# The first expert weights of the odd tiles wait for the first two row gathers, in a decoder step with a grouped mixture of experts

## The chip, the cores and the metric

The kernel runs on one core of one Trainium2 chip. The metric is the device time of one execution in microseconds (us), and lower is better.

## What is computed

One inference step of a one-layer hybrid decoder for 1024 prompt tokens and 32 sample tokens (8 sequences of 4), with a model width of 1024, all in float32. A combined input projection feeds forgetting attention, sparse attention with a window, and an HGRN2 recurrence. An output projection, a residual sum and a layer norm follow. Then comes the part in which the change lies, a grouped top-2 mixture over 16 experts of hidden width 256:

```python
def moe_block(x, router_w, router_bias, w1, w3, w2):
    xf = x.reshape(B * T, D)
    comb = route(xf, router_w, router_bias)        # two experts of one group for each token
    hgt = jnp.einsum('nd,edf->nef', xf, w1)
    hup = jnp.einsum('nd,edf->nef', xf, w3)
    hh = jax.nn.silu(hgt) * hup * comb[..., None].astype(x.dtype)
    return jnp.einsum('nef,efd->nd', hh, w2).reshape(B, T, D)
```

A last residual sum and layer norm give the outputs.

## The kernel before

The program is written out by hand, one instruction stream for each engine, with semaphores between them. SyncE (SP) issues nearly all loads, GpSimd (POOL) issues the stores and the indirect gathers. "arena" in the trace is one large SBUF allocation that holds nearly every tile; "act" and "vec" are rings of PSUM banks, named after the engine that empties them.

The mixture stage computes only the chosen experts. Each token is copied twice, the copies are sorted by expert, and each expert's copies are padded to halves of 64 rows. There are 48 halves, cut into four streams of 12 (`SEG`). A tile is two halves, so there are 24 tiles: an even tile takes one half of stream 0 and one of stream 2, an odd tile one of stream 1 and one of stream 3. Each stream has a slot of its own for the gate and up weights (`Wgu`, 2 MB) and one for the down weights (`Wd`, 1 MB). What each engine does for tile k:

- POOL gathers the tile's 128 token rows of 4 KB from the DRAM tensor `x1_rows` into `xg[k % 2]` (`fetch`, L2035) and counts `x0_loaded` or `x1_loaded` up by 16. `fetch(0)` and `fetch(1)` are issued as soon as DVE has the row numbers (L1903). `fetch(k + 2)` waits until TensorE has turned tile k.
- TensorE turns the rows (`turn_rows`, L1066), eight transposes. It waits for the gather and, from tile 1 on, until ACT (L1322) and DVE (L1920) have emptied the banks of the tile before. It then multiplies by gate and up weights (`gate_up`, L1086, 32 matmuls), which wait for the weights of both streams, and later by the down weights (`down`, L1099).
- TensorE's order is: turn tile 0, turn tile 1, gate_up of tile 0, then in a loop turn tile k + 2, turn the hidden values of tile k, gate_up of tile k + 1, down of tile k. So gate_up of tile 0 stands behind both first gathers, and gate_up of tile 1 needs the weights of streams 1 and 3.

SP's part of it: stream 0 always begins with expert 0, and its three loads go out before the routing is known. The first loads of the other three streams wait until DVE has the expert numbers ("experts known", L1886). `load_gate_up` issues two DMAs of 1 MB, whose contiguous pieces are 1 KB (L437). `load_down` issues one of 1 MB in pieces of 4 KB (L441). The number of the expert is read into a register before (`value_load`, L559). The loads of later steps (`next_gate_up`, `next_down`) are conditional on a change of expert, and wait for `gu_filled` and `dn_filled`, which TensorE counts.

Of the kernel before, what the change touches and what calls it, by code (L numbers as in the profile page):

```python
# [214 lines left out]
def program(nc, ctx, I, O_, known):  # L215
# [194 lines left out]
    def turned_tiles(d):  # L410
# [4 lines left out]
    msem = {n: ctx.enter_context(nc.semaphore(f"moe_{n}")) for n in  # L415
            ("x0_loaded", "x1_loaded", "gu0_loaded", "gu1_loaded", "gu2_loaded", "gu3_loaded", "d0_loaded", "d1_loaded", "d2_loaded", "d3_loaded", "xt_filled", "xt_by_act", "xt_by_vec", "gu_filled", "exp_done",
             "silu_steps", "hidden_done", "ht_filled", "ht_done", "dn_filled", "y_by_act", "y_by_vec", "y0_stored", "y1_stored")}
# [12 lines left out]
    def at_position(stream, j):  # L430

        return bass.ds(j + stream * SEG, 1)

    def load_gate_up(e, stream, expert, **only):
        slot, one = (stream + 1) % 4, bass.ds(expert, 1)
        for dst, src in ((Wgu[:, slot, :, 0:FE], I["exp_w1"]), (Wgu[:, slot, :, FE:], I["exp_w3"])):
            e.dma_start(dst, src[0, one].rearrange("e (c p) f -> p (e c) f", p=P), **only).then_inc(msem[f"gu{stream}_loaded"], 16)  # L437

    def load_down(e, stream, expert, **only):
        slot, one = (stream + 1) % 4, bass.ds(expert, 1)  # L440
        e.dma_start(Wd[:, slot], I["exp_w2"][0, one].rearrange("e (c p) f -> p (e c) f", p=P), **only).then_inc(msem[f"d{stream}_loaded"], 16)  # L441
# [3 lines left out]
    def _(e):  # L445
# [112 lines left out]
        def expert_at(stream, j):  # L558
            return e.value_load(ek_int[0:1, at_position(stream, j)], min_val=0, max_val=NE - 1)  # L559
# [3 lines left out]

        for stream in (2, 1, 3):
            expert = expert_at(stream, 0)
            load_gate_up(e, stream, expert)
            load_down(e, stream, expert)

# [34 lines left out]
    def _(e):  # L603
# [215 lines left out]
        def transposes(d):  # L819
            h, i, kinds = PAIRS[d]  # L820
            e.wait_ge(*E.at(("probs", d)))
            for j, kind in enumerate(kinds):
                _, L, nb = unit_keys(kind, i)
                for a in range(0, nb, 4):
                    e.wait_ge(*E.free("turned"))
                    bk = E.bank("turned")
                    for c in range(min(4, nb - a)):
                        n = min(P, L)
                        last = e.transpose(bk[:n, c * P:(c + 1) * P], score_tiles(d)[j][:, (a + c) * P:(a + c) * P + n], ident)  # L829
                    last.then_inc(*E.filled("turned", ("probs turned", d)))  # L830
# [296 lines left out]
    def _(e):  # L1127
# [131 lines left out]
        for it in range(n + 4):  # L1259
            d = it - 4  # L1260
            if d >= 0 and d % 2:
                h, i, _ = PAIRS[d]
                e.wait_ge(*E.full("summed"))
                bk = E.job("summed")
                e.copy(QT[:, h, i * P:(i + 1) * P], bk[:, 0:P]).then_inc(*E.drained("summed", "prompt attention done"))
            d = it - 2
            if 0 <= d < n:
                h, i, kinds = PAIRS[d]
                for j, kind in enumerate(kinds):
                    _, L, nb = unit_keys(kind, i)  # L1270
                    w = min(P, L)
                    for a in range(0, nb, 4):
                        k = min(4, nb - a)
                        e.wait_ge(*E.full("turned"))
                        bk = E.job("turned")
                        if d >= 2:
                            e.wait_ge(*E.at(("values", d - 2)))
                        e.copy(turned_tiles(d)[j][:w, a:a + k, :], bk[:w, 0:k * P].rearrange("p (c n) -> p c n", c=k)).then_inc(*E.drained("turned", ("pt", d, j)))  # L1278
            if it < n:
                h, i, kinds = PAIRS[it]  # L1280
                for j, kind in enumerate(kinds):
                    _, L, _ = unit_keys(kind, i)
                    e.wait_ge(*E.at(("scores", it, j)))
                    s, sm_ = score_tiles(it)[j][:, 0:L], small[:, it % 4]
                    act(s, s, ACT.Exp, scale=-1.0, bias=sm_[:, least(i, kind, j):least(i, kind, j) + 1], accum_out=sm_[:, j:j + 1]).then_inc(*E.done(("exps", it)))  # L1285
# [805 lines left out]
```

## Time and profile before

| | |
|---|---|
| median of 3 runs | 1565.12 us (1564.02 to 1570.11) |
| profiled execution, its own time | 1562.96 us |
| its span, first to last instruction | 1561.1 us |
| granted TensorE clock, mean over the span | 0.900 of full speed |
| TensorE matmuls busy | 1330.6 us (85%) |
| VectorE, ScalarE, GpSimd busy | 704.5, 376.5, 229.8 us |
| the chain that ended last, by engine | PE 70%, DVE 17%, DMA 4%, POOL 3% |
| mixture stage, from the first dynamic weight load to the last down matmul | 1178.3 to 1487.7 us |

Times in the trace count from the start of the span. The span is 1.9 us shorter than the execution's own time, and the table's median is 2.2 us above that time. The profile gives a DMA issue on SP or POOL as an instruction; how long it takes there is the time to hand the transfer over, and not the transfer. Queue q1 carries what SP issues, queue q0 what POOL issues. A DMA share is the packets' time over that of 16 DMA engines, and can pass 100% since packets overlap.

### The profile page before, as it was taken

The page shows a single profiled execution, that of the slowest core. Times are in us where ns is not written, and L with a number is a line of the kernel's source. Part 1 is how long each engine was busy: PE and PEld are TensorE (multiplying, and loading weights), DVE is VectorE, ACT ScalarE, POOL GpSimd, SP SyncE. Part 2 cuts the span into 40 slices and gives each one's busy share as a digit, 9 for nine tenths or more (in the row PEclk, how much of TensorE's full clock was granted, in tenths as well). Part 3 has the DMA queues.
Part 4 walks back from the last instruction along what each step waited for, and adds up shares of the span by engine and source line. Part 5 has one row for each costly group of instructions (what it writes and reads, how often), then busy time and mean ns, then how long its engine had stood idle before and what let it go on. Part 6 is the DMA issues. An engine that isn't in the chain of part 4 may idle for free.

```text
span 1561.1 us, 19466 instructions
## 1 busy us (share of the span) xinstructions
PE 1330.6 (85%) x7079; PEld 839.1 (54%) x7079; DVE 704.5 (45%) x1543; ACT 376.5 (24%) x817; POOL 229.8 (15%) x251
## 2 busy tenths in 40 slices
PE   2899999999999997899899688599954999999910
PEld 1577777878775555566566577244452333333300
DVE  6444666648541124655555411032643333433359
ACT  3222422324220002566466200000100111111111
POOL 0021030212110003223222100000001111111140
PEclk9799999999999996999999875799956999999965
DMA  9702020301112216000000300701228697595663
GB/s 321 214 1 54 29 55 16 68 1 30 54 42 88 37 18 166 8 23 24 1 2 1 109 0 6 243 0 41 77 102 286 229 323 238 189 314 169 242 222 137
DMA packets 114402, 163.14 MB, mean 105 GB/s; under 512 B 20931, under 2 KB 87667, under 8 KB 114328
## 3 DMA queue, kind: packets, MB, share of 16 engines
q1 hardware_dynamic: 100008, 112.73, 23.7%
q0 software_dynamic: 14320, 49.41, 9.0%
q8 instruction: 48, 0.79, 0.2%
q14 instruction: 26, 0.21, 0.1%
HBM read 225.00 MB, written 36.45 MB: 167 GB/s over the span
## 4 chain that ended last, share of the span: by engine, by line
PE 70%; DVE 17%; DMA 4%; POOL 3%; issue 2%; SPq 2%; ACT 1%; DVEq 0%; POOLq 0%; ACTq 0%
PE act L632 14%; PE vec L1086 10%; PE vec L1030 8%; PE vec L661 6%; PE vec L682 4%; DVE arena L1655 3%; POOL arena L2020 3%; PE vec L817 2%; PE act L841 2%; PE act L829 2%; PE act L1099 2%; PE vec L1099 2%; PE act L1020 2%; DVE arena L1963 1%; DVE arena L1378 1%
## 5 line engine op out<-in xcount | busy, mean ns | idle before, releaser
L632 PE MATMUL act<-arena 128*128 128x352 f32 x768 | 238.9, 467 | 0.4 <-issue 0.4
L632 PEld LDWEIGHTS act<-arena 128*128 128x128 f32 x768 | 145.4, 193 | 77.0 <-issue 3.5
L1086 PE MATMUL vec<-arena 128*64 128x512 f32 x768 | 173.4, 604 | 5.7 <-DMA arena<-in_exp_w 3.0
L1030 PE MATMUL vec<-arena 128*128 128x512 f32 (+1 forms) x288 | 128.1, 607 | 19.0 <-DMA arena<-in_w_out 19.0
L1655 DVE CUSTOM_DVE_ANT_0 arena<-vec,arena 128x128 f32<-128x128 f32 (+9 forms) x200 | 86.9, 458 | 99.8 <-PE vec L817 89.7
L1086 PEld LDWEIGHTS vec<-arena 128*64 128x64 f32 x768 | 54.7, 138 | 107.7 <-issue 107.3
L1030 PEld LDWEIGHTS vec<-arena 128*128 128x128 f32 (+1 forms) x288 | 52.7, 184 | 92.2 <-issue 91.3
L661 PE MATMUL vec<-arena 128*128 128x512 f32 (+1 forms) x256 | 99.9, 546 | 0.0
L817 PE MATMUL vec<-arena 64*128 64x512 f32 (+11 forms) x352 | 86.5, 491 | 2.5 <-DVE arena L1655 2.0
L1278 ACT COPY arena<-act 128x512 f32<-128x512 f32 (+11 forms) x176 | 63.5, 432 | 101.4 <-PE act L829 101.4
L2020 POOL TENSOR_SCALAR arena<-arena 128x640 f32<-128x640 f32 (+4 forms) x64 | 59.9, 947 | 185.6 <-DVE arena L1667 185.6
L1926 DVE TENSOR_SCALAR arena<-arena 128x256 f32<-128x256 f32 x24 | 7.1, 296 | 176.0 <-ACT arena L1328 176.0
L1285 ACT ACTIVATE arena<-arena 128x640 f32<-128x640 f32 (+15 forms) x128 | 81.6, 645 | 11.6 <-DVE arena L1655 11.5
L829 PE MATMUL act<-arena 128*128 128x128 f32 (+4 forms) x440 | 66.1, 287 | 21.0 <-POOL arena L2020 19.6
L661 PEld LDWEIGHTS vec<-arena 128*128 128x128 f32 x256 | 47.8, 190 | 44.9 <-issue 27.7
L829 PEld LDWEIGHTS act<-arena 128*128 128x128 f32 (+4 forms) x440 | 47.1, 142 | 43.1 <-POOL arena L2020 23.6
L682 PEld LDWEIGHTS vec<-arena 128*128 128x128 f32 x512 | 61.9, 192 | 9.3 <-DVE arena L1472 3.2
L1489 DVE COPY_PREDICATED arena<-arena,vec 128x512 f32<-128x512 int32 x64 | 44.7, 732 | 48.3 <-PE vec L682 46.5
L642 PE MATMUL vec<-arena 128*128 128x128 f32 (+1 forms) x576 | 65.3, 275 | 0.0
L642 PEld LDWEIGHTS vec<-arena 128*128 128x128 f32 (+1 forms) x576 | 64.5, 183 | 1.3
L682 PE MATMUL vec<-arena 128*128 128x128 f32 x512 | 62.7, 276 | 2.4 <-DVE arena L1472 2.4
L817 PEld LDWEIGHTS vec<-arena 64*128 64x128 f32 x352 | 43.3, 203 | 35.6 <-issue 24.7
(363 smaller groups left out, 1942.5 us busy)
## 6 DMA issues: line engine op xcount, KB each, us to landing
arena<-in_exp_w SPq DMA_DIRECT2D x144, 1024.0 KB
y_rows<-arena POOLq DMA_DIRECT2D x48, 256.0 KB, 5.3
arena<-in_w_in SPq DMA_DIRECT2D x16, 512.0 KB, 7.0
arena<-in_x_prompt SPq DMA_DIRECT2D x8, 512.0 KB, 10.4
x_spill<-arena POOLq DMA_DIRECT2D x8, 512.0 KB, 4.0
arena<-in_cache_fox_kv SPq DMA_DIRECT2D x16, 256.0 KB, 3.0
arena<-x_spill SPq DMA_DIRECT2D x8, 512.0 KB, 17.9
x_rows<-arena POOLq DMA_DIRECT2D x8, 512.0 KB, 3.6
```

What stands on the lines that cost most here:

```text
L632: last = mm(bk[:, 0:n], W[k % 2][:, c, m * P:(m + 1) * P], xT[:, c, a:a + n], start=c == 0, stop=c == NC - 1)
L642: last = mm(bk[:r, o:o + P], xT[:, c, t * P:t * P + r], W[h % 2][:, c, 3 * P:4 * P], start=c == 0, stop=c == NC - 1)
L661: last = mm(bk[:r, 0:width], xT[:, c, t * P:t * P + r], w[:, c, 0:width], start=c == 0, stop=c == NC - 1)
L682: last = mm(bk[:, c * P:(c + 1) * P], a[:, ch], b[:, ch], start=True, stop=True)
L817: mm(bk[:, 0:n], QT[s, h, i * P:(i + 1) * P], k[:, first + a:first + a + n], start=True, stop=True).then_inc(*E.filled("vec"))
L829: last = e.transpose(bk[:n, c * P:(c + 1) * P], score_tiles(d)[j][:, (a + c) * P:(a + c) * P + n], ident)
L1030: last = mm(bk[:r], src, Wo[:, c, half * 512:(half + 1) * 512], start=c == 0, stop=c == NC - 1)
L1086: last = mm(gu_bank[p][o], xgT[p][:, c, o], Wgu[:, slot, c, :], start=c == 0, stop=c == NC - 1)
L1278: e.copy(turned_tiles(d)[j][:w, a:a + k, :], bk[:w, 0:k * P].rearrange("p (c n) -> p c n", c=k)).then_inc(*E.drained("turned", ("pt", d, j)))
L1285: act(s, s, ACT.Exp, scale=-1.0, bias=sm_[:, least(i, kind, j):least(i, kind, j) + 1], accum_out=sm_[:, j:j + 1]).then_inc(*E.done(("exps" ...
L1655: ins = e.tensor_tensor_reduce(out=s[:, a + o:a + o + w], in0=bk[:, o:o + w], in1=bias, scale=1.0, scalar=prior, op0=ALU.add, op1=ALU.min, ...
L2020: e.tensor_scalar(s, s, small[:, d % 4, 2 + j:3 + j], None, ALU.mult).then_inc(*E.done(("probs", d)))
```

## The change

After it has read stream 1's expert number and before it issues stream 1's loads, SP waits for the landing of the gathers of tile 0 and of tile 1. The order is stream 2, stream 1, stream 3, so the loads of stream 2 go out as before and the six loads of streams 1 and 3 stand behind the wait.

```diff
         for stream in (2, 1, 3):
             expert = expert_at(stream, 0)
+            if stream == 1:
+                e.wait_ge(msem["x0_loaded"], 16)
+                e.wait_ge(msem["x1_loaded"], 16)
             load_gate_up(e, stream, expert)
             load_down(e, stream, expert)
```

## Rows read from the trace of the kernel before

**Rows 1.** Windows by stage: us, busy time per engine (instructions), PEclk, DMA share, GB/s.
```profile
1178.00:1211.00 33.00, 16.01 (x96) 8.96 (x98) 8.94 (x21) 2.52 (x5) 4.00 (x4) 0.66 1.00 349
1211.00:1482.00 271.00, 268.00 (x1313) 101.28 (x1311) 95.28 (x133) 42.80 (x89) 43.88 (x64) 0.99 0.72 244
1482.00:1561.10 79.10, 5.11 (x24) 1.39 (x20) 59.61 (x72) 9.88 (x14) 21.93 (x22) 0.56 0.51 177
```

**Rows 2.** Timeline of SP: start us, us, engine, line, operation.
```profile
1178.27 1.03 SPq L437 DMA_DIRECT2D arena<-in_exp_w  x2
1179.39 1.77 SPq L441 DMA_DIRECT2D arena<-in_exp_w  x1
1181.92 5.84 SPq L437 DMA_DIRECT2D arena<-in_exp_w  x2
1192.88 6.15 SPq L437 DMA_DIRECT2D arena<-in_exp_w  x2
```

**Rows 3.** Timeline of POOL and PE at the first two tiles, idle time in brackets.
```profile
1182.36 1.17 POOL L2035 DMA_INDIRECT arena<-x_rows,arena  x1 [44.45 <-DVE arena L1903]
1183.83 0.96 POOL L2035 DMA_INDIRECT arena<-x_rows,arena  x1 [0.30 <-issue]
...
1190.63 1.11 PE L1066 MATMUL act<-arena 128*128 128x128 f32 x4 [8.85 <-DMA arena<-x_rows,arena]
...
1193.55 1.09 PE L1066 MATMUL act<-arena 128*128 128x128 f32 x4 [0.95 <-DVE arena L1920]
...
1195.42 5.07 PE L1086 MATMUL vec<-arena 128*64 128x512 f32 x18
```

**Rows 4.** Landing of the first gather, then of the first two together.
```profile
DMA to landing us min/median/max: 8.2/8.2/8.2
...
DMA to landing us min/median/max: 8.2/8.4/8.5
```

**Rows 5.** DMA queues in 1179:1187, 1187:1192, 1179:1192, 1192:1212: packets, MB, share.
```profile
q1 hardware_dynamic: 2193, 2.56, 98.1%
...
q0 software_dynamic: 288, 1.05, 52.9%
...
q1 hardware_dynamic: 2691, 3.49, 79.5%
...
q1 hardware_dynamic: 4363, 5.94, 86.9%
```

**Rows 6.** Chain that ended last, in order of time: start us, us, what.
```profile
1193.36 16.89 DMA arena<-in_exp_w
...
1210.50 9.06 PE vec L1086 x32
```

**Rows 7.** Windows around the start and the end of the transfers.
```profile
1179.00:1180.00 1.00, 0.35 (x7) 0.35 (x8) 0.93 (x3) 0.00 (x0) 0.00 (x0) 0.50 0.51 83
1180.00:1181.00 1.00, 1.00 (x24) 1.00 (x23) 0.06 (x1) 0.00 (x0) 0.00 (x0) 0.50 0.80 250
1181.00:1182.00 1.00, 0.78 (x16) 0.65 (x14) 0.11 (x1) 0.00 (x0) 0.00 (x0) 0.50 1.10 389
...
1192.00:1210.00 18.00, 12.01 (x53) 5.26 (x51) 4.88 (x7) 2.35 (x5) 1.87 (x2) 0.78 1.07 372
...
1208.00:1210.00 2.00, 0.00 (x0) 0.00 (x0) 0.00 (x0) 0.00 (x0) 0.00 (x0) 0.50 1.04 396
1210.00:1214.00 4.00, 3.50 (x10) 1.18 (x12) 0.00 (x0) 0.00 (x0) 0.00 (x0) 0.50 0.20 80
```

**Rows 8.** Timeline of PE: gate_up of tile 1, and of a later tile.
```profile
1210.50 1.98 PE L1086 MATMUL vec<-arena 128*64 128x512 f32 x4 [3.04 <-DMA arena<-in_exp_w]
...
1247.59 7.10 PE L1086 MATMUL vec<-arena 128*64 128x512 f32 x32
```

**Rows 9.** A gather issued on empty queues, and queue q0 in 1495:1496.
```profile
1493.91 1.02 POOL L2062 DMA_INDIRECT arena<-y_rows,arena  x1 [3.95 <-DMA y_rows<-arena]
...
q0 software_dynamic: 18, 0.07, 64.9%
```

## Prediction

> **What bounds the kernel now.** I read the stages first, in a table of windows. In the tile loop TensorE is busy for 268.0 of 271 us [rows 1]. The stretch behind it is left to DVE and the gathers, and nothing in it was loaded ahead, so it starts when the tiles end. Ahead of the loop lies the one stretch that the change touches, 33 us in which the DMA engines are at a share of 1.00 and TensorE at half [rows 1]. The reader is to see that in the loop each us by which gate_up of tile 1 comes later or earlier is carried to the end.
>
> The chain that ended last says what releases tile 1: from 1193.36 us it follows one transfer of expert weights for 16.89 us, and then gate_up [rows 6]. The timeline of PE says the same from the other side: 3.04 us idle, ended by that DMA [rows 8]. So the question is when the weights of streams 1 and 3 have landed, and the start of tile 0 counts for nothing so long as it is done before.
>
> Then the transfers. The loads behind stream 2's three are handed over from 1181.92 us on, and a pair of them keeps SP for 5.84 or 6.15 us where stream 2's first pair took 1.03 us [rows 2]: the queue is full. The table of DMA queues tells what moved when. From 1179 to 1192 us, q1 moved 3.49 MB. Stream 2's three loads are 3.15 MB, so 0.34 MB of stream 1 moved as well. From 1192 to 1212 us it moved the other 5.94 MB of the nine loads (9.44 MB) [rows 5]. The two first gathers, 1.05 MB, moved between 1187 and 1192 us [rows 5].
>
> **What the change does, step by step.**
>
> *Removed contention.* The hope of such a wait is an earlier landing of the gathers. Stream 2's loads stay ahead of them. Up to 1187 us q1 moved 2.56 MB, all of it stream 2's, and the gathers had moved nothing though they were issued at 1182.36 and 1183.83 us [rows 3, 5]. Up to that time the change alters no transfer. From 1187 to 1192 us q1 moved 3.49 - 2.56 = 0.93 MB, of which 3.15 - 2.56 = 0.59 MB is still stream 2's. Only the 0.34 MB of stream 1 goes away. It moved at the end of this stretch, so the first gather, which landed 8.2 us after its issue (1190.6 us) [rows 4], gains next to nothing. The second landed 8.5 us after its issue, at about 1192.4 us [rows 4]. It can gain at most what all of the 0.34 MB takes at the stretch's rate of (1.05 + 0.93) / 5 = 0.40 MB/us, which is 0.9 us. Much of it moved after the gathers' last data, so I take 0.3 us and a landing at 1192.1 us.
>
> *Tile 0.* TensorE turned tile 0 at 1190.63 us when the gather had landed. It turned tile 1 at 1193.55 us, released by DVE's copy L1920, and not by the second gather [rows 3]. So a second gather that lands 0.3 us earlier moves nothing there: gate_up of tile 0 stays at 1195.4 us, within 0.3 us. What it would be worth is nothing in any case, since TensorE then waits for weights.
>
> *Added wait on SP.* SP holds at the wait from about 1181.9 us, where it now issues stream 1's first load [rows 2], to 1192.1 us. Behind the wait stand the six loads of streams 1 and 3, and then SP's later steps. These wait for gate_up of tile 0 anyway, which ends 7 to 9 us after its start at 1195.42 us [rows 3, 8], and none of their data moves before tile 1 is done (the DMA share falls to 0.20 from 1210 us) [rows 7]. POOL's gathers of tiles 2 and 3 hang on TensorE's turns, which stay.
>
> *What the delay of 10.2 us costs.* Most of it is work that stood in a queue anyway. The cost is the time in which the queue runs dry, plus what stream 1 had moved by then.
> 1. The handing over: 0.3 us from the semaphore to the first issue (my estimate, from POOL's gap of 0.30 us between two issues [rows 3]; the expert's number is read before the wait). Issue at 1192.4 us.
> 2. The start-up of an empty queue. Stream 2's first issue was at 1178.27 us [rows 2]. The windows then show 83, 250 and 389 GB/s, 0.72 MB by 1182 us [rows 7]. At 0.37 MB/us that is 1.95 us of full flow, so flow starts in effect at 1180.05 us, 1.8 us after the issue. Here: 1194.2 us.
> 3. At 1192 us before, 0.34 MB of stream 1 had moved, 0.9 us at 0.37 MB/us. The state of 1192.0 us is reached at 1194.2 + 0.9 = 1195.1 us.
>
> From there the same bytes remain, in the same order, 5.94 MB beside the gathers of tiles 2 and 3, at the 372 GB/s of that stretch [rows 5, 7]. So the last gate and up load lands 3.1 us later, and gate_up of tile 1 starts at 1213.6 instead of 1210.50 us.
>
> One page of the Trainium skill gives this gap another size: "DMA: Bandwidth & Descriptors", section "Anatomy of one DMA", puts setup and completion handling together at about 2.0 us of fixed cost. By it the gap between the gathers' last data and the new flow would be 2.0 us and the sum perhaps 1 us smaller. No row here shows the two ends of that gap in a single number.
>
> *The clock.* gate_up of tile 1 takes 9.06 us, that of a later tile 7.10 us [rows 6, 8]. The difference of 1.96 us is the granted clock at 0.50 (1.2 of 2.4 GHz) after the idle time: it is there in 1208 to 1210 us and until 1214 us [rows 7]. In the change TensorE idles for 6.1 instead of 3.04 us. The clock has already fallen in the shorter idle time, so the longer one adds nothing: 0, and at most 0.3 us.
>
> **Sum.** -0 (gathers) +3.1 (weights of tile 1) +0 (clock) = +3.1 us. Bounds: at least +1.9 us, if the second gather gains its full 0.9 us and the handing over takes nothing; at most +3.8 us, if it gains nothing and the clock costs 0.3 us, with 0.1 us more of handing over. The profiled execution's own time would go from 1562.96 to 1566.1 us, its span from 1561.1 to 1564.2 us. The median of the runs shown is 2.2 us above that execution, 1565.12 us, and so 1568.2 us.
>
> **The rivals.**
>
> *A, the gathers come sooner and the gap closes: no change.* A gather on empty queues, issued at 1493.91 us, had packets moving within 1495 to 1496 us, under 2.1 us after its issue [rows 9]; the first one of tile 0 needed over 4.6 us, from 1182.36 us to past 1187 us [rows 3, 5]. If what held it up is the handing over of stream 1's loads, whose first pair kept SP for 5.84 us just then [rows 2], and not stream 2's 1 KB pieces, the change lets it start at about 1184.5 us. Both gathers would then move beside stream 2, land by about 1189 us, and SP would issue at 1189.3 us. Stream 2 and the gathers, 4.2 MB, keep the engines busy from 1180.05 us to 1191.3 us at 0.37 MB/us, and the new flow starts at 1191.1 us. No gap, and a shift of 0: 1565.1 us. Against it: the gathers began when stream 2's 2.1 MB in small pieces were through, which 2.56 MB by 1187 us puts at 1186 us. The same page of the Trainium skill, section "Queues, rings and completion order", says that each DMA engine goes round between the queues that have work. By that rule the gathers should share from the start. The trace disagrees up to 1187 us, where q0 moved nothing, and agrees behind it, where both moved 1 MB.
>
> *B, faster: the weights of tile 1 come without the wait.* If less mixing let the transfers run better, TensorE would lose neither the 3.04 us nor the 1.96 us of low clock: -5.0 us, 1560.1 us at best. It needs the nine loads and four gathers, 11.5 MB, to end 3 us sooner out of some 31 us, a tenth more throughput. The pieces stay what they are and the engines were at a share of 1.07 [rows 7], so little speaks for it.
>
> *C, slower by more than can be measured from no change.* If a load took as long from its issue as now, because its time is its own and not that of the queue ahead (16.89 us for the last one that counts [rows 6]), the whole delay of 10.2 us would pass on: 1575.3 us. It decides from 7.8 us of shift on. Against it: q1's transfers ran without a break until 1210 us, so most of the 16.89 us was spent behind others.
>
> **How the numbers follow.** A measurement of this kernel tells about 0.5% (7.8 us) from no change. Chances: forecast 0.68, A 0.18, B 0.06, C 0.08. The likeliest case alone gives 1567.0 to 1569.0 us. The range for 8 in 10 takes in A and the spread of the runs before (1564.0 to 1570.1 us) and leaves out C and most of B: 1563.0 to 1571.0 us. Only C passes 7.8 us, and in part: 0.06 slower. B alone stays below it, so faster needs luck as well: 0.02. The rest is 0.92.
>
> **What would show it.** In the profile after: no SP load between 1181.2 and about 1192.4 us; a window near 1192 to 1193.5 us with a DMA share well under 1, which is the gap; the issues of stream 1 short, since the queue is empty; q0's first packets again at about 1187 us (at 1184 to 1185 us under A); gate_up of tile 0 at 1195.4 us and of tile 1 at about 1213.6 us with some 6 us idle ahead of it and about 9.1 us long; 7.10 us for gate_up of the later tiles, unchanged. The prediction is wrong if the gap is missing, if tile 1's weights land outside 1212.4 to 1214.3 us, or if the shift is given back in the loop.

## The result, and the profile after

The changed kernel is slower by a little. Over 20 runs each, the ratio of its time to that of the kernel before is 1.0032, with a 95% interval of 1.0017 to 1.0047: 5.0 us (2.7 to 7.4) on 1565.16 us. The median of its own 20 runs is 1571.93 us, 0.9 us above the stated range, while the ratio gives 1565.16 x 1.0032 = 1570.2 us. The same kernel in a second comparison had a ratio of 1.0017 (0.9999 to 1.0036). Single runs of either kernel scatter by 12 us (1561.86 to 1573.79 us for the kernel before, 1564.40 to 1576.42 us for the changed one), so the medians say little about a change of 3 us. The trace says more.

In the profiled execution after, the first gather is issued at 1188.20 us, 5.84 us later than before, and up to there the order of the work is the same. So both traces are read from that issue on, and I write "at +x us" for x us behind it. The timeline of PE in the changed kernel (start us, us, engine, line, operation, idle time before) answers to [rows 3, 8]:

```profile
1196.23 1.11 PE L1069 MATMUL act<-arena 128*128 128x128 f32 x4 [8.62 <-DMA arena<-x_rows,arena]
...
1199.15 1.09 PE L1069 MATMUL act<-arena 128*128 128x128 f32 x4 [0.95 <-DVE arena L1923]
...
1201.02 8.27 PE L1089 MATMUL vec<-arena 128*64 128x512 f32 x32
...
1219.49 9.26 PE L1089 MATMUL vec<-arena 128*64 128x512 f32 x32 [6.24 <-DMA arena<-in_exp_w]
```

gate_up of tile 0 starts at +12.82 us (+13.06 before), that of tile 1 at +31.29 us (+28.14 before, 1210.50 - 1182.36 [rows 3, 8]). That is 3.15 us later, and the idle time ahead of it has grown from 3.04 to 6.24 us. The timeline of SP in the changed kernel shows the wait and what it did to the issues, against [rows 2]:

```profile
1185.23 1.83 SPq L441 DMA_DIRECT2D arena<-in_exp_w  x1
1198.10 1.00 SPq L437 DMA_DIRECT2D arena<-in_exp_w  x2
1199.20 1.48 SPq L441 DMA_DIRECT2D arena<-in_exp_w  x1
1201.43 7.88 SPq L437 DMA_DIRECT2D arena<-in_exp_w  x2
```

Stream 1's first pair is handed over in 1.00 us, where it took 5.84 us: the queue was empty. The windows of the changed kernel (PEclk, DMA share and GB/s are the last three columns) show for how long:

```profile
1196.00:1197.00 1.00, 0.77 (x4) 0.77 (x5) 0.00 (x0) 0.00 (x0) 0.00 (x0) 0.50 0.76 303
1197.00:1198.00 1.00, 1.00 (x6) 0.80 (x4) 0.00 (x0) 0.56 (x1) 0.00 (x0) 0.50 0.02 8
1198.00:1199.00 1.00, 0.20 (x1) 0.00 (x0) 0.69 (x1) 0.03 (x1) 0.53 (x1) 0.50 0.00 0
1199.00:1200.00 1.00, 0.85 (x4) 0.88 (x5) 0.00 (x1) 0.00 (x0) 0.41 (x1) 0.50 0.44 98
1200.00:1201.00 1.00, 1.00 (x6) 0.69 (x4) 0.00 (x0) 0.59 (x1) 0.00 (x0) 0.50 0.89 257
1201.00:1202.00 1.00, 1.00 (x5) 0.36 (x6) 0.69 (x1) 0.00 (x0) 0.63 (x1) 0.50 1.07 381
```

The kernel before had no such hole: it moved 373 GB/s from 1188 to 1198 us, which is from +5.6 to +15.6 us. Here 8, 0 and 98 GB/s stand in three windows: the gathers' data was through, and their landing, SP's issue and the start of the next loads went by. No packet at all moved from 1197.5 to 1199.1 us. The DMA queues of the changed kernel from 1184 to 1198 us and from 1198 to 1220 us, packets, MB and share:

```profile
q1 hardware_dynamic: 2352, 3.15, 65.1%
q0 software_dynamic: 288, 1.05, 18.8%
...
q1 hardware_dynamic: 4695, 6.26, 82.8%
q0 software_dynamic: 288, 1.05, 12.5%
```

Up to 1198 us (+9.8 us) q1 moved stream 2 and no byte more. The kernel before had moved 3.49 MB by +9.6 us [rows 5].

What this cost can be read in bytes. All queues together, from 6 us ahead of the first gather's issue to 20 us behind it, moved this much before (1176.36 to 1202.36 us) and after (1182.2 to 1208.2 us):

```profile
DMA packets 5350, 8.45 MB, mean 325 GB/s; under 512 B 151, under 2 KB 4337, under 8 KB 5349
...
DMA packets 4921, 7.29 MB, mean 280 GB/s; under 512 B 130, under 2 KB 4150, under 8 KB 4920
```

The changed kernel is 1.16 MB behind, which at 0.37 MB/us is 3.1 us.

### The profile page after: what moved, and what is told of

Same layout as the page of the kernel before. It is cut to its first block, busy times and chain, and to the rows that moved or that the text cites. A ratio compares the mean times of both kernels' runs of the same rounds, so it can differ in the third digit from the quotient of the medians.

```text
span 1570.5 us, 19467 instructions
## 1 busy us (share of the span) xinstructions
PE 1334.8 (85%) x7079; PEld 840.5 (54%) x7079; DVE 704.6 (45%) x1543; ACT 377.1 (24%) x817; POOL 230.4 (15%) x251
## 4 chain that ended last, share of the span: by engine, by line
PE 70%; DVE 17%; DMA 5%; POOL 3%; issue 2%; SPq 1%; ACT 1%; DVEq 0%; POOLq 0%; ACTq 0%
PE act L635 14%; PE vec L1089 10%; PE vec L1033 8%; PE vec L664 6%; PE vec L685 4%; POOL arena L2023 3%; DVE arena L1658 3%; PE vec L820 3%; PE act L844 3%; PE act L832 3%; PE act L1102 2%; PE vec L1102 2%; PE act L1023 1%; DVE arena L1966 1%; DVE arena L1381 1%
```

## The experiments

For each experiment I read the same marks from the profile: the start and length of gate_up of tile 1, the idle time ahead of it, and the time from the first gather's issue to the first gather of the results (L2062 in the kernel before), called the stage. "Moved" is what all queues together moved from 6 us ahead of the first gather's issue to 20 us behind it. Each row's marks come from one profile; its ratio comes from all its runs. The diffs are against the changed kernel where nothing else is said.

| kernel | SP issues stream 1 at | moved, MB | idle, us | gate_up of tile 1 at | its length, us | stage, us | ratio (95% interval) |
|---|---|---|---|---|---|---|---|
| before, first profile | -0.44 | 8.45 | 3.04 | +28.14 | 9.06 | 311.5 | 1 |
| before, second profile | -0.44 | 8.44 | 3.17 | +28.23 | 8.97 | 311.7 | |
| changed, first | +9.90 | 7.29 | 6.24 | +31.29 | 9.26 | 315.0 | 1.0032 (1.0017 to 1.0047) |
| changed, second | +10.03 | 7.25 | 6.21 | +31.24 | 9.22 | 315.9 | 1.0017 (0.9999 to 1.0036) |
| two waits long satisfied | -0.38 | 8.44 | 3.21 | +28.53 | 9.07 | 312.6 | 0.9997 (0.9980 to 1.0014) |
| waits before stream 3 | -0.32 | 8.44 | 3.20 | +28.27 | 8.97 | 311.5 | 0.9991 (0.9973 to 1.0009) |
| wait for the first gather only | +8.21 | 7.99 | 4.36 | +29.34 | 8.44 | 312.1 | 1.0025 (1.0009 to 1.0041) |
| third wait, for the turns | +13.23 | 6.53 | 7.87 | +33.08 | 8.49 | 316.6 | 1.0021 (1.0003 to 1.0039) |
| waits before stream 2 | +10.89 | 5.24 | 5.42 | +36.79 | 9.83 | 320.9 | 1.0073 (1.0049 to 1.0096) |
| down loads last, no wait | -1.78 | 7.74 | 0 | +24.85 | 8.80 | 307.7 | 0.9963 (0.9947 to 0.9979) |
| down loads last, with the waits | +8.42 | 6.76 | 2.98 | +27.43 | 9.39 | 311.2 | 0.9993 (0.9977 to 1.0010) |

In all these kernels but the last two the nine loads go out in one order, and there the bytes and the delay go together. The kernels with a dry queue are 0.46, 1.16, 1.20, 1.92 and 3.21 MB behind the first profile before. At 0.37 MB/us that is 1.2, 3.1, 3.2, 5.2 and 8.7 us, and gate_up of tile 1 came 1.20, 3.15, 3.10, 4.94 and 8.65 us later. The two kernels whose waits left the queue full are level with it, at 8.44 MB. The ratios are too coarse to order the doses: 1.0025, 1.0032 and 1.0021 for waits that end at +8.2, +9.9 and +13.2 us.

**The kernel before once more.** No edit.

> The kernel before once more, for a second profile, to see what its own mixture stage scatters by. Theory (the scatter of single runs comes from the stages ahead of the mixture): gate_up of tile 1 again 28.1 to 28.4 us after the first gather's issue, and 311.5 to 312.6 us to the first gather of the results, wherever the first gather's issue itself falls. Rival (the stage itself scatters by several us): gate_up of tile 1 more than 1 us away from 28.1 us.

Its first gather was issued at 1189.11 us, 6.75 us later than in the first profile, and the marks behind it are within 0.2 us of the first profile's. So the scatter of single runs comes mostly from the stages ahead of the mixture, and 5.84 us of the 9.4 us between the two first spans (1561.1 and 1570.5 us) need no part of the change.

**The changed kernel once more.** No edit.

> The changed kernel once more, for a second profile and a second comparison. Theory: from the first gather's issue to the first gather of the results, 3.1 to 3.6 us longer than in the kernel before (311.5 us there, 315.0 us in the first profile), gate_up of tile 1 31.3 us after the first gather's issue (28.1 us before), ratio 1.002 to 1.003. Rival (something in the stages ahead costs 1 to 2 us as well): ratio again 1.003 or above with the same 315 us.

The start of gate_up of tile 1 repeats within 0.05 us. The stage is 4.3 us longer than in the first profile before, and not 3.4 us as the first time, so it missed the 3.1 to 3.6 us expected. The difference arose in the loop behind gate_up of tile 1, which took 275.4 us here and 274.4 us there; over all the kernels of the table it took 274.0 to 275.4 us. The ratio's interval does not decide between the 1.002 to 1.003 expected and the rival's 1.003 or above.

**Two waits that cost no time.** Against the kernel before:

```diff
+            if stream == 1:
+                e.wait_ge(*E.at("x1 stored"))
+                e.wait_ge(*E.at("x1 stored"))
```

> Two waits at the place of the change on a semaphore that has long reached its value (the landing of the x1 rows in DRAM, some 40 us earlier). The program has the same number of instructions as the changed one. Theory (the cost is the 3.1 us dry queue and a bit of clock, the rest of the measured 5 us is scatter of the stages ahead): same time as before, ratio 1.000 within 0.1%. Rival (the added instructions move something in the stages ahead by 1 to 2 us): ratio 1.001 or above, and the first gather issued later than in the kernel before in the profile.

No difference in the ratio, and no hole: the extra instructions are not the cost. The rival's second mark, a later issue of the first gather, did appear (1187.39 us against 1182.36 us), but the kernel before had it at 1189.11 us itself in its second profile.

**The waits one stream later.**

```diff
-            if stream == 1:
+            if stream == 3:
```

> The same two waits, moved one stream later: stream 2 and stream 1 are issued as before, and only stream 3's three loads wait for the gathers. Theory (the cost is the time in which q1 runs dry, not the delay of the issue): before, SP handed stream 3's first load over at 1192.88 us and the second gather landed at about 1192.4 us, so the wait is over when SP arrives, the queue never runs dry, and nothing moves: shift 0, ratio to before 1.000, TensorE idle ahead of gate_up of tile 1 about 3.0 us. Rival (a wait for the gathers costs something of its own, or the extra instructions move the stages ahead): slower by 2 us or more, ratio 1.0015 or above.

No mark moved by more than 0.2 us. With stream 1 in the queue, SP reaches the wait when the gathers have landed, at +10.63 us it issues stream 3 (+10.52 before), and the queue stays full.

**A wait for the first gather only.**

```diff
             if stream == 1:
                 e.wait_ge(msem["x0_loaded"], 16)
-                e.wait_ge(msem["x1_loaded"], 16)
```

> Stream 1 waits for the first gather alone. Theory (dry queue): the first gather lands 1.8 us ahead of the second, so SP issues about 1.6 us sooner than with both waits, and the dry time shrinks by as much: gate_up of tile 1 comes 1.5 us later than before instead of 3.1 us, idle ahead of it 4.6 us, ratio about 1.001. Rival (the loss is contention or something else that any wait brings): the same 3.1 us as with both waits.

The dose follows: SP issues 1.7 us sooner than with both waits, and gate_up of tile 1 starts 2.0 us sooner, 1.2 us later than before. That is read from one profile. Its stage is only 0.6 us longer than before, since gate_up of tile 1 took 0.6 us less there, at a higher granted clock. The ratio of 1.0025 (1.4 to 6.4 us) does not meet these 0.6 us, so some of what the runs lost lies outside the stage or differs from run to run; which, stays open.

**A longer wait.**

```diff
                 e.wait_ge(msem["x1_loaded"], 16)
+                e.wait_ge(msem["xt_filled"], 4)
```

> A third wait behind the two: SP also waits until TensorE has turned the rows of tiles 0 and 1, some 3.2 us after the second gather's landing. Theory (once the queue is dry, each further us of waiting is one us of delay): stream 1 is issued about 13.2 us after the first gather's issue instead of 9.9 us, gate_up of tile 1 at 34.5 us instead of 31.3 us, ratio about 1.004. Rival (a fixed price for breaking the stream of loads, whatever its length): gate_up of tile 1 stays near 31.3 us.

SP issues 3.33 us later than in the changed kernel, and gate_up of tile 1 only 1.79 us later. Neither the slope of one nor the fixed price holds. What filled part of the dry time is in the queues of this kernel from 1200 to 1203 us, where only one of them has a row:

```profile
q0 software_dynamic: 115, 0.46, 49.1%
```

The third gather, issued by POOL at +10.38 us, moved 0.46 MB on empty engines. That is work which the changed kernel does later, beside the weights: 0.46 / 0.37 = 1.2 us, and 3.33 - 1.2 = 2.1 us is near the 1.79 us measured. This was worked out after the run, and the bytes moved bear it out (6.53 against 7.29 MB, 2.1 us). A us of waiting costs a us only so long as nothing else moves in it.

**The waits ahead of stream 2.**

```diff
-            if stream == 1:
+            if stream == 2:
```

> The same two waits ahead of stream 2, so that no dynamic weight load stands ahead of the gathers and they run on empty queues. It tells what held the first gather's packets back for 4.6 us after its issue. If it was q1's load: first packets of q0 1.5 to 2 us after the issue, the second gather landed about 5.5 us after the first one's issue. If the 4.6 us are GpSimd's own at this place: first packets again 4.6 us after the issue, with empty engines. For the time: all nine loads start after the landing, q1 has 9.44 MB to move instead of 5.94 MB at 1192 us; gate_up of tile 1 comes 8 to 11 us later than before, gate_up of tile 0 some 3 us later; ratio about 1.006 and clear of noise.

The gathers run on empty queues. The landing of the first gather, then of both, from issue, and queue q0 in 1185 to 1186 us (the issue is at 1183.66 us, and q0 and q1 have no packet up to 1185 us):

```profile
DMA to landing us min/median/max: 4.5/4.5/4.5
...
DMA to landing us min/median/max: 4.5/4.9/5.3
...
q0 software_dynamic: 18, 0.07, 56.8%
```

The first gather's packets start 1.3 to 2.3 us after its issue and it lands after 4.5 us, where it took 8.2 us before [rows 4] and 8.0 us in the changed kernel. So it is q1's load that holds it up, and the load of stream 2 alone is enough, as the changed kernel shows. The second gather landed 6.8 us after the first one's issue (I had said 5.5 us). The price is as expected for gate_up of tile 1, 8.7 us later than before; gate_up of tile 0 came 5.8 us later (I had said 3 us).

**The down loads last.** Against the kernel before:

```diff
-        for stream in (2, 1, 3):
-            expert = expert_at(stream, 0)
+        firsts = [(stream, expert_at(stream, 0)) for stream in (2, 1, 3)]
+        for stream, expert in firsts:
             load_gate_up(e, stream, expert)
+        for stream, expert in firsts:
             load_down(e, stream, expert)
```

> No wait; the gate and up weights of streams 2, 1 and 3 go first and the three down loads last. Theory (gate_up of tile 1 waits for bytes in a full queue, of which 2.1 MB, the down weights of streams 2 and 1, are not needed yet): these weights land 5 us sooner, TensorE finds them there, the 3.0 us of idle time ahead of gate_up of tile 1 go, and the clock does not fall, 2.0 us more: gate_up of tile 1 at 25.1 us after the first gather's issue and 7.1 us long, ratio 0.997. Rival (the small pieces of 1 KB ahead of and beside the gathers hold these back): the first gather lands later than 8.2 us after its issue, gate_up of tile 0 starts later, and half or more of the gain is lost.

This one beats both kernels: 0.9963 (0.9947 to 0.9979), 5.8 us by the ratio and 3.9 us in the stage. The timeline of its PE:

```profile
1210.58 0.27 PE L1074 MATMUL act<-arena 128*128 128x128 f32 x1
1210.78 8.80 PE L1087 MATMUL vec<-arena 128*64 128x512 f32 x32
```

gate_up of tile 1 follows the turn of the hidden values with no wait for weights, and the first gather lands sooner and not later (the turn of tile 0 at +7.36 us, +8.27 before). So the start is 3.3 us sooner by two things together: the 3.0 us of idle time are gone and the gather came 0.9 us sooner, less 0.7 us by which gate_up of tile 0 took longer (8.81 us, 8.08 before). The idle time went as expected, the clock did not: gate_up is 8.80 us long. The windows of this kernel show the granted clock falling all the same:

```profile
1207.00:1209.00 2.00, 0.92 (x8) 0.68 (x7) 1.61 (x2) 0.91 (x2) 0.00 (x0) 1.00 1.08 386
1209.00:1211.00 2.00, 0.59 (x4) 0.40 (x6) 1.89 (x4) 0.11 (x1) 0.00 (x0) 1.00 1.04 413
...
1213.00:1215.00 2.00, 2.00 (x7) 0.49 (x5) 0.00 (x0) 0.00 (x0) 0.00 (x0) 0.50 1.04 416
```

TensorE was busy for 1.51 of the 4 us ahead, with the turns and the wait for DVE's silu between them, and the clock is at 0.50 (1.2 GHz) in the middle of gate_up. Only 0.26 of the 1.96 us came back.

**The down loads last, with the waits.** The order above, with the two waits of the change between stream 2's and stream 1's gate and up loads.

> The same order with the down loads last, and the two waits of the change between the gate and up loads of stream 2 and of stream 1. Theory: the queue runs dry as in the changed kernel, but the 2.1 MB of down loads that now lie behind leave 5 us of cover, so the dry time costs gate_up of tile 1 1 us or less against the order without the waits; ratio 0.998. Rival (the waits cost their 3 us in any order): gate_up of tile 1 some 3 us later than without them, and no gain over the kernel before.

My theory missed. I expected the 2.1 MB behind to cover the dry time, and gate_up of tile 1 to come 1 us later at most than without the waits. It came 2.58 us later, with 2.98 us of idle time for weights, so the rival is right: the waits cost their 3 us in this order too. The landing records of stream 3's gate and up loads in the traces say it without TensorE. The last of them stands at +27.89 us before and +31.05 us in the changed kernel, and at +24.00 us with the down loads last and +27.18 us with the waits added: 3.16 us later in one order, 3.18 us in the other. The cover was what I had wrong. Without the waits the weights landed at +24.00 us and gate_up began at +24.85 us. It begins 0.25 us after the landing where it waits for it, so the cover was 0.60 us and not 5 us, and 3.18 - 0.60 = 2.58 us is what was measured. Moving 2.1 MB behind brought the landing forward by 3.9 us, and 3.3 us of that were used up by TensorE's earlier start. Against that order without them, the waits cost 1.0030 in ratio (0.9993 / 0.9963) and 3.5 us in the stage.

## Why the prediction was right or wrong

*The main step, the dry queue, was right in place and size.* Forecast: SP's next issue at 1192.4 us in the times of the first trace, which is +10.0 us; measured +9.90 us. Flow in effect from 1.8 us after it; measured, 0.74 MB had moved by 1202 us, 2.0 us of flow at 0.37 MB/us, so from 1200.0 us, 1.9 us after the issue. gate_up of tile 1 3.1 us later; measured 3.15 us and, in the second profile, 3.10 us. The control with satisfied waits and the waits before stream 3 show that the wait alone costs nothing where the queue stays full, and the bytes moved follow the delay over five profiles with a dry queue, from 1.2 to 8.7 us.

*The removed contention was small, as forecast, and just as useless.* The second gather landed 0.3 us sooner, at +9.7 us by the chain of waits (issue 1189.67 us plus 8.22 us), and I had said +9.7 us (1192.1 us). The first landed 0.2 us sooner. The start of tile 0 moved by 0.24 us, and TensorE then waited 3.2 us longer for weights.

*The clock* had been put at 0 to 0.3 us, and gate_up of tile 1 took 0.20 and 0.16 us longer in the two profiles. That is within the bound. But the length went from 8.44 to 9.83 us over the table without following the idle time, so the 0.2 us can't be put to the longer idle time, and that so little came of it here is in part luck.

*The sum.* I forecast +3.1 us; the stage has +3.4 and +4.3 us against the first profile before (+3.3 and +4.2 us against the second), the ratios 5.0 us (2.7 to 7.4) and 2.7 us (-0.2 to 5.6). All four agree with a loss of 3.3 to 4.3 us. The first ratio's middle lies above the sum's upper bound of 3.8 us; what the step of the sum leaves out is the loop behind, 0.1 and 1.1 us longer than in the first profile before, which I had taken as exactly the same. The kernels without any dry queue scatter there as well (274.0 to 275.0 us), so I do not put this to the change. The lower bound counts 0.3 us twice: the +3.1 us already hold a gain of 0.3 us by the second gather, so a gain of 0.9 us and no handing over give +2.2 and not +1.9 us. The ratio's 1570.2 us lies above the 1567.0 to 1569.0 us of the likeliest case; that it lies in the range for 8 in 10 is owed to the spread of single runs that the range allowed for.

*Rival A* (the gathers start sooner and close the gap) fell. In the changed kernel SP hands nothing over from 1187.1 us on, and q0 had moved 3 packets by 1193 us, over 4 us after the issue, as before. Its premise was half right: a load on q1 does hold the gathers back, 8.0 us to landing against 4.5 us on empty queues, but stream 2's own loads are enough for it. The Trainium skill's rule of queues taking turns ("DMA: Bandwidth & Descriptors", section "Queues, rings and completion order") does not show in these 4 us of any trace here, only behind them. The rule speaks of the queues that a DMA engine has work for. No trace here tells whether the gathers' work had reached the DMA engines in these 4 us, so the prediction's "the trace disagrees" was too strong. The 2.0 us of fixed cost on the same page of the Trainium skill (section "Anatomy of one DMA", where it is given for a DMA that GpSimd issues) is near the time in which no packet moved, 1.7 us from the gathers' last packet to q1's first. But the loss was not 1 us below the forecast, as the prediction worked out from that figure: the flow had thinned out before (213 GB/s in the half us before 1197 us) and was full only from 1201 us on.

*Rival B* (better flow) fell: 369 GB/s from 1200 to 1218 us, 372 GB/s before [rows 7]. *Rival C* (the whole delay passes on) fell: 10.3 us of later issue made 3.15 us, since most of a load's time from issue to landing is spent behind others.

## What to carry to other kernels

A wait that keeps loads out of the way of a small transfer costs nothing while the queue behind it is still full, and costs the time from that transfer's last bytes to the next load's full flow once the queue runs dry: here 3 us for one pair of waits, in either order of the loads. Before adding one, count the bytes left in the queue when the wait ends, and ask whether the sooner transfer starts anything that is not waiting for the delayed bytes too. Where a stage waits for bytes in a full queue, the order of the bytes is the better lever: moving loads that are needed later behind those needed first gave 4 us in the stage and 5.8 us (3.3 to 8.3) by the ratio here, without any wait. Count the cover that such an order leaves from when the engine would start, and not from the bytes moved behind: of 5 us expected here, 0.6 us were there.

## What the runs showed of the hardware that was not expected

- The first indirect gather of 512 KB lands 4.5 us after its issue on empty queues, 8.0 to 8.2 us behind stream 2's three loads, and 7.0 and 7.3 us in the two orders with the down loads last. Most of the difference lies ahead of its first packet (1.3 to 2.3 us after the issue against over 4 us). The third gather shows the same: its packets began 1.6 us after its issue where the queues were empty (1199.62 to 1201.2 us, with the third wait). It holds too when the other load is only just starting: with the waits ahead of stream 2, the third gather was issued at 1190.50 us, before q1's first packets, and its own came after 1194 us. What in the queue does this stays open.
- The length of gate_up of tile 1 does not grow with the idle time ahead of it: 8.44 us after 4.36 us, 9.06 us after 3.04 us, 9.26 us after 6.24 us, 8.49 us after 7.87 us, and 8.80 us after none at all. It follows the granted clock over its own length, which was 0.84, 0.78, 0.76, 0.83 and 0.81 in these five: length times clock is 7.0 to 7.1 us each time, the 7.10 us of a later tile.
- The stages ahead of the mixture scatter by 6.9 us between profiles of the same or nearly the same program (first gather issued from 1182.36 to 1189.26 us). The kernel before covers nearly all of that by itself (1182.36 and 1189.11 us), so it needs no part of any change here.
